# Seven block products instead of eight in the first feed-forward stage of a hybrid encoder, with its filter work moved between the output products

## What is computed

```python
def swiglu(x, w_in, w_out):
    gate, up = jnp.split(x @ w_in, 2, axis=-1)
    return (jax.nn.silu(gate) * up) @ w_out

def encoder_layer(x, lp):
    x = x + 0.5 * swiglu(rms_norm(x, lp['norm_ffn1']), lp['ffn1_w_in'], lp['ffn1_w_out'])
    h = rms_norm(x, lp['norm_mix'])
    proj = h @ lp['w_in']
    ...                        # RWKV-7 scans, 2-D neighbourhood attention, long Hyena filters
    x = x + mixed @ lp['w_out']
    x = x + 0.5 * swiglu(rms_norm(x, lp['norm_ffn2']), lp['ffn2_w_in'], lp['ffn2_w_out'])
    return x
```

## Time and profile before

| | us |
|---|---|
| median of 3 runs | 3453.22 (3447.7 to 3457.7) |
| the profiled execution | 3456.03 |
| its span, first to last instruction | 3454.2 |
| PE busy | 3322.5 (96%) |
| DVE busy | 2113.3 (61%) |
| ACT busy | 1153.1 (33%) |

### The profile page before, as it was taken

One profiled execution on the slowest core, in us unless ns is written; L12 is line 12 of the kernel. 1 busy time (PEld: TensorE's weight loads), 2 busy tenths in 40 slices (PEclk: granted clock), 3 DMA queues, 4 the chain that ended last, 5 costly groups with the idle time before them and its releaser, 6 DMA issues.

```text
span 3454.2 us, 61563 instructions
## 1 busy us (share of the span) xinstructions
PE 3322.5 (96%) x26092; PEld 3125.4 (90%) x26092; DVE 2113.3 (61%) x3792; ACT 1153.1 (33%) x2015; POOL 50.4 (1%) x62
## 2 busy tenths in 40 slices
PE   7999999999998999999999999999999979999998
PEld 7999999888776899999999999998887768999997
DVE  5443444663878686666754534456548886776666
ACT  4221213221445353333431212132224544443333
POOL 0000000000000000000000000000000000000000
PEclk9999999999999999999999999999999999999999
DMA  3122121222033222222222121222310512222221
GB/s 136 61 78 69 61 74 56 104 96 85 4 115 137 68 62 73 72 68 68 69 77 80 63 84 48 73 88 78 106 59 5 197 54 80 65 69 72 71 68 67
DMA packets 80770, 264.36 MB, mean 77 GB/s; under 512 B 8994, under 2 KB 8994, under 8 KB 79216
## 3 DMA queue, kind: packets, MB, share of 16 engines
q1 hardware_dynamic: 76944, 248.08, 21.9%
q0 software_dynamic: 3552, 12.34, 1.1%
HBM read 230.50 MB, written 29.88 MB: 75 GB/s over the span
## 4 chain that ended last, share of the span: by engine, by line
PE 88%; DVE 8%; issue 2%; DMA 1%; ACT 1%; SPq 0%; DVEq 0%; ACTq 0%
PE ps L896 70%; PE ps L1033 18%; DMA gtab<-hyc 1%; DVE rstd L2107 0%; DVE uv L2735 0%; DVE sc L2785 0%; DMA bias<-bias 0%; DMA x<-xT 0%; PE ps L1489 0%; DVE M2X L2508 0%; ACT mh L2024 0%; DVE wl L2267 0%; DVE Mrk L2495 0%; DVE hout L2893 0%; DVE ktok L2496 0%
## 5 line engine op out<-in xcount | busy, mean ns | idle before, releaser
L896 PE MATMUL ps<-hh,wh 128*128 128x384 f32 (+2 forms) x2112 | 717.3, 340 | 11.5 <-DVE hl L2115 10.4
L896 PE MATMUL ps<-hl,wh 128*128 128x384 f32 (+2 forms) x2112 | 708.8, 336 | 0.0
L896 PE MATMUL ps<-hh,wl 128*128 128x384 f32 (+2 forms) x2112 | 708.4, 335 | 0.0
L896 PE MATMUL ps<-act_high,wh 128*128 128x384 f32 x1408 | 471.3, 335 | 1.7 <-DVE act_low L2313 1.7
L896 PE MATMUL ps<-act_high,wl 128*128 128x384 f32 x1408 | 470.4, 334 | 0.0
L896 PE MATMUL ps<-act_low,wh 128*128 128x384 f32 x1408 | 470.4, 334 | 0.0
L1624 ACT CAST wh<-wring 128x1024 fp32r<-128x1024 f32 (+3 forms) x300 | 261.7, 888 | 573.9 <-PE ps L896 541.6
L896 PEld LDWEIGHTS ps<-hh,wh 128*128 128x128 f32 x2112 | 398.8, 189 | 35.3 <-issue 16.0
L1033 PE MATMUL ps<-gh,wh 128*128 128x384 f32 x1232 | 414.1, 336 | 12.6 <-DVE gated L2284 4.3
L2146 DVE SCALAR_TENSOR_TENSOR x<-ps,x 128x384 f32<-128x384 f32 x320 | 177.4, 556 | 391.1 <-PE ps L896 390.9
L1033 PE MATMUL ps<-gh,wl 128*128 128x384 f32 x1232 | 412.9, 335 | 0.0
(11 more groups left out here) (305 smaller groups left out, 4642.1 us busy)
## 6 DMA issues: line engine op xcount, KB each, us to landing
wring<-wa SPq DMA_DIRECT2D x244, 512.0 KB, 3.5
wring<-wa SPq DMA_DIRECT2D x64, 320.0 KB, 2.8
wring<-wa SPq DMA_DIRECT2D x32, 384.0 KB, 3.1
bias<-bias SPq DMA_DIRECT2D x24, 512.0 KB, 8.3
wring<-wa SPq DMA_DIRECT2D x48, 256.0 KB, 2.5
conv_q_k<-stage SPq DMA_DIRECT2D x28, 384.0 KB, 2.6
kern_rows<-kst POOLq DMA_DIRECT2D x12, 512.0 KB, 3.3
outT<-x SPq DMA_DIRECT2D x2, 3072.0 KB, 10.3
```

The lines of the kernel that those rows point to most:

```text
L896: return pe.matmul(out, lhsT, rhs, start=start, stop=stop)
```

## The change

- The first feed-forward stage uses the seven-product scheme too: `ffn_pairs(l, f)` with f = 0 or 1 takes the place of both.
- Both stages have six blocks: 3, 3, 4, 4, 4, 4.
- The split ring is half as large (4 half tiles, `RING`). The other half of the space holds filter data in the first stage. Units and output tiles are one list of items, and each is split `LEAD` = 3 items ahead.
- The filter products stand between output products, each filter job in two halves of 128 channels (`CHH`), spaced by `filter_places`; one table buffer instead of two, loads and weights in halves, 12 stores a layer of 256 KB each with rows of 128 elements.
- The first norm of the program has its squares summed by PE in PSUM (`first_norm`), tile by tile, behind product 5 of the first pair; the first pair's token sums are made by `start` for all tiles at once.
- The last output tiles of the second stage come in `M_ORDER`, and the token sums for the next layer's first stage are made there.

```diff
-FF_BLOCKS = [[(0, 6), (6, 6), (12, 5), (17, 5)], [(0, 5), (5, 5), (10, 4), (14, 4), (18, 4)]]
+FF_BLOCKS = [(0, 3), (3, 3), (6, 4), (10, 4), (14, 4), (18, 4)]
-UNITS = 7
-HALVES = 2 * SPLITS
+UNITS, RING, LEAD = 7, 4, 3
...
+            def first_norm():
+
+                pe.wait_ge(s_const, 16)
+                for m in range(KT):
+                    pe.wait_ge(s_sq, m + 1)
+                    for f in range(2):
+                        got = mm(bank(6 + f, HALF), cs("ones"), sqb[:, m % 2, f * HALF:(f + 1) * HALF], m == 0, m == KT - 1)
+                    got.then_inc(s_first, 1)
...
+                        product(l, f, j, 4)
+                        product(l, f, j, 5)
+                        if J == 0:
+                            first_norm()
                         pe.wait_ge(s_exit, 4 * J + 2)
-                        product(l, j, 6)
+                        product(l, f, j, 6)
...
                             m.then_inc(s_fo, 1)
+                            if f == 0:
+                                filters(l, v)
...
                     pe.wait_ge(*fa.at(l, "sin", 2))
+                    pe.wait_ge(s_hz, 64 * l + 48 + 16 * h)
...
+                        first_gate(J, ba)
+                        items_to(l, f, q + 4 + LEAD)
+                        second_up(J, ba)
+                        items_to(l, f, q + 5 + LEAD)
+                        second_gate(J, ba)
+                        items_to(l, f, q + 6 + LEAD)
+                        gate_up(J, 1)
...
+                        if last and m:
+                            if more:
+                                pair_done(2 * l + 2, m - 1)
+                            else:
+                                x_done(None if f else "norm_mix", m - 1)
+                        if last and more and m >= OUT_TILES - 2:
+                            if m == OUT_TILES - 2:
+                                items[0] = 0
+                            items_to(l + 1, 0, m - (OUT_TILES - 2))
...
             for l in L:
                 cap_b = use_base(l, 2) - 1
                 derive()
-                norm()
-                ffn(l, cap_b)
-                ve.wait_ge(s_kst, 96 * (l + 1))
+                ffn_pairs(l, 0)
+                ve.wait_ge(s_kst, 16 * STORES * (l + 1))
```

More of the change, by code:

```diff
@@ L464, in k_fa @@
             out = []
-            for u in sorted(FILTER_AT):
-                job = FILTER_AT[u]
-                out += {"mlp": [("sin", job[1])], "taps": [("abs", job[1], job[-1] + i) for i in range(2)], "sum": [],
-                        "kern": [("odd",) + job[1:]]}[job[0]]
+            for job in FILTER_JOBS:
+                out += {"mlp": [("sin", job[1])], "sum": [], "kern": [("odd",) + job[1:]],
+                        "taps": [("abs",) + job[1:3] + (job[-1] + i,) for i in range(2)]}[job[0]]
             return out
@@ L919, in h_k, with filters @@
                 return hh[:, c, cols], hl[:, c, cols]
-            def filters(l, unit, block):
+            def filters(l, unit):
                 job = FILTER_AT.get(unit)
@@ L1707, in hold, with items_to @@
+            items = [0]
+            def items_to(l, f, q):
+                while items[0] <= q < len(FF_ITEMS):
+                    if FF_ITEMS[items[0]][0] == "unit":
+                        unit_high(l, f, items[0])
+                    else:
+                        split[0] = out_tile(l, f, items[0])
+                        split_to(split[0])
+                    items[0] += 1
+            def hold(l, f, j, i):
+                J = stage_pair(l, f, j)
                 sa.wait_ge(s_prod, UNITS * J + i + 1)
@@ L1751, in ffn_pairs @@
[L1751 to L1764 removed]
+                            act_high1(l, f, b, j - 1, 1)
@@ new lines, in ffn_pairs @@
+                        for i in range(UNITS):
+                            items_to(l, f, q + LEAD)
+                            q += 1
+                            if i < 3 and not begun:
+                                hold(l, f, j, i)
+                            if i == 0 and j > j0:
+                                act_high1(l, f, b, j - 1, 0)
+                            if i == 2 and j == 0 and not begun:
+                                norm()
+                            if i == 4:
+                                silu_of(l, f, j, 0)
@@ new lines, in ffn_pairs @@
+                        if f == 0:
+                            for v in range(2):
+                                filters(l, 16 * b + 2 * m + v)
+                ready = x_count(l, f) + FF_OUTS
+                if more:
+                    pair_done(2 * l + 2, OUT_TILES - 1, ready)
+                    items_to(l + 1, 0, LEAD - 1)
+                elif f:
+                    square(OUT_TILES - 1, ready, M_ORDER[-1])
+                else:
+                    x_done("norm_mix", OUT_TILES - 1, ready)
@@ L2844, in _ @@
             ve.memset(eps[:, 1:2], GN_EPS).then_inc(s_eps, 1)
[L2845 to L2854 removed]
+            start()
             ve.wait_ge(s_const, 16)
```

1161 lines of the change are left out of this document (571 added, 590 removed).

## The result

| | before | changed | ratio (95%) |
|---|---|---|---|
| median of 15 runs, us | 3451.17 | 3460.46 (3457.3 to 3465.0) | 1.0025 (1.0018 to 1.0032) |
| the profiled execution | 3456.03 | 3460.43 | |
| its span | 3454.2 | 3458.6 | |

The change makes the kernel 9.3 us slower, 0.27%; 3440 was forecast, 0.3% faster. The measured time lies inside the range, but the sign is wrong. The span grew by 4.4 us only, because the profiled execution of before is 4.9 us above its median of 15 runs.

What follows compares the result with a forecast made beforehand. PE was taken to bound the kernel. Of 91.5 us off PE most comes back: second layer's first stage -14.0, first layer's -5.9, second stages +7.0, sum -12.9, so 3440 us against the median; range 3414 to 3463.

Steps and rivals of the forecast that it cites:

- Products, -91.5 us: First feed-forward stages: 264 fewer matrix instructions a layer at 0.1733 us, 45.8 us off PE per layer, 91.5 in all.
- The pair's margin, 0.45 us: In each pair, the second up ends about 0.45 us before PE wants it for product 6; move costed at nothing.
- the rival of the missed margin: Raw tiles land late, second up ends 0.45 us after PE wants it in 64 pairs: +29, 3469 us; chance 0.11.
- The start, pair's end at 63: Program's first pair, behind DVE's token sums and the norm's squares, ends near 63 us; first layer's first stage -5.9.
- a cheap start: Rival: first pair ends at 53, transition costs nothing more, filters do not wait: 3417 us; chance 0.17.
- Filters' narrow instructions, +5.3 a layer: First stages: filter instructions of 256 columns become twice as many of 128, 39.2 us becoming 44.5 a layer.
- Waits for filters, +5.5: First stages, filter jobs between output products: 4 us a layer for the `hwt` load, 1.5 for other job chains.
- Blocks, +2.5 and +1.9: Six blocks for five, with two short ones: +2.5 us in a first stage, +1.9 in a second.
- From layer to layer, +7.3: Second feed-forward stage into the next layer's first: DVE falls behind by 2.1 us per two output tiles, +7.3 us.
- Second stages, +3.5 each: Each second stage: 1.9 us for blocks, 1.6 in the first pair from later unit splits; +7.0 for both.
- The base: Median of the kernel before, taken as 3453.22 us; the profiled execution's 3456.03 stood 2.8 above it.
- filters come late: Rival: with DVE busier, every filter job waits 0.25 us more, 66 times, 16.5 us: 3456 us; chance 0.19.

Runs made afterwards that it cites:

- Run 12: Changed kernel with four reorderings together (3424.9), plus ACT rounding unit 6 ahead of the norm's root in the first pair of three stages: 3420.8 us, ratio 0.9918.
- run 7: Changed kernel with the first weight sum of every pair made twice by DVE, to measure the second up's margin: 3503.2 us, ratio 1.0152.
- run 1: Changed kernel with the first norm's squares made by ACT as x lands and summed by PE ahead of product 0: 3448.2 us, ratio 0.9989.
- Run 4: Kernel before the change with only its second stages put in six blocks, 3, 3, 4, 4, 4, 4: 3468.3 us, ratio 1.0042.
- run 11: Changed kernel, DVE adding squares of tiles 2 to 7 for only 8 of 768 tokens at three transitions, part of the norm left out: 3451.6 us, ratio 1.0004.
- run 9: Changed kernel with the squares' additions for tiles 1 to 7 moved from DVE to POOL in three transitions: 3463.1 us, ratio 1.0032.

## Why the prediction was wrong

The step that failed is the price of waiting. The sum took each idle time of PE at its length and put the lower clock behind it at 2 us for the program's start and at nothing elsewhere; the products at half pace came to 16.1 us more over the kernel, about what the whole sum missed (17.3). Beside it four terms were too small: the program's start, the odd start of a block (not in the sum), the transition between the layers and the second stages.

- *Products, -91.5 us.* Right, and the pair's pace too. Run 12 keeps a third of it.
- *The pair's margin, 0.45 us.* Right in sign and size, so the rival of the missed margin did not come. In the changed kernel's rows above, the second up ends at 1379.13 and product 6 of that pair is due at 1367.18 + 6 x 2.08 = 1379.66, 0.53 us later; less the 0.06 us between DVE's end and PE's start in run 7 it is 0.47, the margin that run 7 gives.
- *The start, pair's end at 63.* It ended at 66.4, and with the half pace that goes on into the next pair the two pairs behind it end as if it had been 66.9 (96.00 less two of 14.56), 3.9 later. The order of the terms was read rightly: product 5 ended at 44.7 for 42.5, the sixteen sums took 10.5 for 8.6. The terms of the first figure sum to 14.3 + 22.0 + 6.7 = 43.0 for DVE alone, so its 42.5 for PE was too early by its own sum; the second came from a row whose fourth instruction is overlapped by the next product (1.07 us for four), while 32 in a row stand 0.33 apart at a granted clock of 1.00. What was not seen is that the squares were the cause and not a part: without them there, 15.5 us go (run 1). The rival "a cheap start" at 53 is what a better order gives. (It read the earlier trace rows as showing no other idle time above 1 us in the block stage; the PE timeline of before has waits of 1.28 and 1.44 us in the first pair.)
- *Filters' narrow instructions, +5.3 a layer.* 6.0 and 6.4 measured, from 38.2 to 44.2 and 44.6. The 47.5 us with gaps that the sum had come out near 50.5. The 312 instructions of 128 columns of a layer took 0.133 us each on the mean, and 0.112 within a group. The 81 ns of the Trainium skill (TensorE: Matmul & The Clock Gate, section "Back-to-back issue gap") did not hold here; the earlier trace rows did.
- *Waits for filters, +5.5.* The wait for `hwt` was forecast at 4 and is 2.9, the load landing in 3.8 us; the 2.3 us estimated by the formula of the Trainium skill (DMA: Bandwidth & Descriptors, section "Anatomy of one DMA") was too short. The waits for taps, 1.2 us a layer, are near the 1.5 put for them. (The jobs are 34 a layer and not 33.) What failed is that an idle time was priced by its length. Behind these four waits PE ran at half pace, 5 to 10 instructions and up to 1.5 us at a time, so the wait of 1.2 us for taps in block 0 cost 2.7.
- *Blocks, +2.5 and +1.9.* The waits for `act_low` at the block ends came out as in the sum: 2.8 us a stage, 1.9 more than the 0.9 before. The odd start's wait of 2.25 us in the first stages was not in it; in the kernel before such a start waited 0.70, and the order shows it (PE waits for `s_xup` at odd tiles). Run 4 shows that the estimate was wrong for the old item list by a factor of three.
- *From layer to layer, +7.3.* The first pair took 34.0 us from the last output product where 24.3 stood behind the mixing: 9.7. The mechanism, DVE's queue behind the last output tiles, was right, as run 11 shows; 31 of the pair's instructions stand at half pace, 8 behind the mixing before, which is 3.4 us of the 9.7.
- *Second stages, +3.5 each.* 5.5 and 6.3. The first pair lost 2.5 and 2.3 for 1.6, and the block ends the 1.9 of the sum; the rest is in waits and half pace of under 1 us each.
- *Projections and mixing.* They came out 3.1 and 3.3 us shorter, in small steps over the scans, the attention and the Hyena part. The variants of the changed kernel spread over 4 us there, and all lie below the kernel before (598.1 and 597.2). Nothing was forecast there, and the cause stays open.
- *The base.* 3453.22 was the median of three runs; that of 15 is 3451.17.

In sum 17.3 us were missed in the span: 9.3 at the start and in the first layer's first stage, 9.6 in the second layer's, 4.8 in second stages, less 6.4 in the stretches between. Most terms were off by 1 to 4 us, nearly all to the same side; the half pace was missing as a term. That the time still lies in the stated range owes 6.4 us to the stretches between, for which nothing was forecast: that is luck. The case "filters come late", at 3456, is the nearest of those forecast, though with another mechanism.

## What to carry to other kernels

A change that takes work from the bound engine and gives DVE and ACT more should be priced with each idle time it makes at its length plus the half pace behind it, taken from a row that shows both. Even a wait of 0.25 us cost 0.50 here, once it came in every pair (run 7). Work that is not needed soon (a norm's squares) must not stand in a queue ahead of work that the next product needs, above all if it waits for that same product. Where a sum of small terms gives 0.4%, look for the mending moves in the same trace: four reorderings, each a line or a few, were worth 36 us here, more than the change itself promised.

## What the runs showed of the hardware

An addition of 128 x 768 by POOL took 1.84 us at its quickest and up to 4.94 with DVE at work, and two of DVE's operations beside it went from 0.61 to 1.24 and 2.18 us (run 9): the two engines hinder each other, and work moved from one to the other is not free. It does not fall on all operations: seven of DVE's, begun and ended within POOL's addition at 1738.69, kept their 0.54 to 0.68 us. POOL in run 9:

```profile
1223.92 4.94 POOL L946 TENSOR_TENSOR rstd<-rstd,sqb 128x768 f32<-128x768 f32 x1 [6.03 <-ACT sqb L1694]
...
1722.67 1.84 POOL L946 TENSOR_TENSOR rstd<-rstd,sqb 128x768 f32<-128x768 f32 x1 [0.96 <-ACT sqb L1694]
```

Not every idle time of PE is followed by the lower clock. One of 1.19 us, with eight narrow filter products right behind it, was followed 1.8 us after its end by ten instructions at 0.32 us, with a granted clock of 0.50, the lower level of 1.2 GHz. One of 2.43 us in a first pair (at 1237.53), between full-width products, was followed by ten as well, while one of 2.25 us at a block's start (at 133.93), also between full-width products, was followed by none. What decides it, no run shows. Timeline of PE in block 0:

```profile
120.28 1.21 PE L981 MATMUL ps<-hwt,h 64*128 64x128 f32 x8 [1.19 <-DVE taps L2246]
121.42 0.44 PE L981 MATMUL ps<-act_high,wh 128*128 128x384 f32 x1
...
122.39 0.52 PE L981 MATMUL ps<-act_low,wh 128*128 128x384 f32 x1
122.71 0.52 PE L981 MATMUL ps<-act_high,wl 128*128 128x384 f32 x1
```
